# Expert rows fetched in pairs: one indexed DMA for U and V, shared slots, and coefficients for every two picks

## The chip, the cores and the metric

The kernel runs on one core of one Trainium2 chip. Its time is the device time of one execution in microseconds (us), the median of several. A profiled execution is one more execution, with a trace of every instruction and every DMA packet. The engines are TensorE (PE, its weight loads apart as PEld), VectorE (DVE), ScalarE (ACT), GpSimd (POOL) and SyncE (SP). DMA work is done by 16 DMA engines.

## What is computed

Two blocks of layers over 256 tokens of width 1024. The first block has two layers, each a mixer (a gated delta rule in layer 0, attention in layer 1) followed by an expert layer. The change touches only the expert layers:

```python
def peer(h, w_query, sub_keys, u_tab, v_tab):
    def block_fn(xb):                                   # 128 tokens
        qry = (xb @ w_query).reshape(P, PEER_HEADS, 2, PEER_HALF)
        s = jnp.einsum('phcd,hckd->phck', qry, sub_keys)
        top_s, top_i = lax.top_k(s, PEER_TOPK)          # 16 of 128 keys, twice
        cand_s = top_s[..., 0, :, None] + top_s[..., 1, None, :]
        cand_i = top_i[..., 0, :, None] * 128 + top_i[..., 1, None, :]
        best_s, pos = lax.top_k(cand_s.reshape(P, 8, 256), PEER_TOPK)
        idx = jnp.take_along_axis(cand_i.reshape(P, 8, 256), pos, axis=-1)
        gate = jax.nn.softmax(best_s, axis=-1)
        act = jax.nn.gelu(jnp.einsum('pd,phkd->phk', xb, u_tab[idx]), approximate=False)
        return jnp.einsum('phk,phkd->pd', gate * act, v_tab[idx])
```

Each token picks 16 experts in each of 8 heads out of 16384. A pick is a row of 1024 float32 of U (4 KB), which is multiplied with the token, and the row of V with the same number, which is added to the sum with a coefficient. U and V are 64 MB each a layer; only the picked rows are read.

## The kernel before

The class `Peer` (line 1356) is one expert layer. It runs twice: `peer_a` over four tiles of 128 tokens (512 tokens, context and latents) and `peer_m` over two. A **unit** is one tile and one head, so there are 32 and then 16 units; a unit has 16 **picks**, and pick g = 16u + s is one gather of 128 rows (one a token) of U and one of V. In all there are 768 picks, 512 KB of U and 512 KB of V each.

Every engine has its own program; they meet at semaphores. For one unit u:

- **VectorE** (`dve`, 1622; `dve_choose`, 1703) chooses the experts of unit u + 2 in 14 small steps, which stand between the dot products of unit u. `dve_dot` (1657) multiplies a U row with the token and sums it (line 1664). `dve_coef` (1667) makes the 16 coefficients of a unit at once from softmax and gelu; it runs after the third dot of the next unit.
- **ScalarE** (`act`, 1519): softmax's exp of unit u + 2 (1587), gelu of all 16 dots of unit u (1545), then 16 diagonal matrices, the identity scaled with a column of coefficients (1551). Between the diagonals it copies what TensorE made for later units (1571, 1575, 1581).
- **TensorE** (`pe_sum`, 1501): for each pick two matmuls of the diagonal with the V row (1515), which add up in two PSUM banks over the tile's eight units. Between them stand the steps of `between`: the transposes of a token tile ("h", line 212), the query products of two chunks ("q", 8 matmuls each, 1473) and the scores against the keys ("s", 1486). They stand in units 0 to 7 of the first expert layer (512 columns in units 0 to 3, 384 after) and 0 to 5 of the second.
- **GpSimd** (`pool`, 1588) issues the gathers: `pool_u` (1604) for pick s of unit u + 1, then `pool_v` (1612) for pick s of unit u, in turn. U rows go to 7 slots of 4 KB a partition, free again after the dot; V rows go to 7 other slots, free again after the matmul. The indices are ready two units ahead. The last three V slots hold the norm's scratch at first, so V's fifth gather waits for the norm of all tiles.
- **SyncE** loads the query weights (1 MB for two chunks) into a ring.

At the start of a layer VectorE takes the norm, chooses unit 0, does six steps of choosing unit 1 and begins with the dots. ScalarE and TensorE do the norm of tile 0, query chunks 0 to 3, the norm of the rest, chunks 4 to 7, and then the units. At the end of a tile `dve_add` (1677) adds the sum to the residual.

## Time and profile before

| | us |
|---|---|
| median of 3 runs | 4846.64 |
| lowest, highest | 4842.84, 4847.74 |
| profiled execution, first to last instruction (its span) | 4732.4 |
| first gather to last sum of `peer_a` | 1381 to 2826 |
| first gather to last sum of `peer_m` | 3009 to 3723 |

| engine | busy, us | share of the span |
|---|---|---|
| TensorE matmul | 3897.4 | 82% |
| VectorE | 2747.9 | 58% |
| GpSimd | 2127.3 | 45% |
| ScalarE | 883.1 | 19% |

For the profiled execution itself there is the span alone; the runs' median lies 114 us above it. Busy shares are averages over stages with different limits, so they are read per stretch. A row of a table of stretches gives the busy time of each engine, the granted TensorE clock as a share of 2.4 GHz, the mean busy share of the 16 DMA engines (it goes a little over 1 where packets overlap) and what they moved.

### The profile page before, as it was taken

What the parts mean: (1) busy time and instruction counts of PE and PEld (TensorE: products, weight loads), DVE (VectorE), ACT (ScalarE), POOL (GpSimd) and SP (SyncE); (2) the same over time, 40 slices, a digit from 0 to 9 for tenths busy, and PEclk for the clock granted to TensorE, in tenths of its full rate; (3) what the DMA queues carried; (4) which work ended last, traced back from release to release, by engine and by line L of the source; (5) the groups of instructions that cost most, each with busy time, mean ns of one, the idle gap of its engine ahead of it and who ended that gap; (6) DMA issues with size and microseconds to landing.
All of it is one profiled execution on the core that took longest, in us unless ns stands there. A gap on an engine that the chain in (4) does not pass through costs nothing.

```text
span 4732.4 us, 41731 instructions
## 1 busy us (share of the span) xinstructions
PE 3897.4 (82%) x14279; PEld 2202.3 (47%) x14279; DVE 2747.9 (58%) x5596; ACT 883.1 (19%) x2101; POOL 2127.3 (45%) x1999
## 2 busy tenths in 40 slices
PE   6799999899978987777777778688777889875999
PEld 1448864598644443322222235444322357532584
DVE  1258872678646666666666635666666247538241
ACT  0233221332212221111111112222111111010100
POOL 1006430255217777777777760377777300018000
PEclk6699999999989999988988999899898889986999
DMA  9310002100149999999999981799999524320343
GB/s 371 126 61 1 1 27 71 54 1 1 44 152 376 378 376 376 391 385 384 406 391 383 386 328 54 255 402 405 404 390 400 204 82 133 129 93 1 121 149 124
DMA packets 380097, 1043.15 MB, mean 220 GB/s; under 512 B 31683, under 2 KB 115885, under 8 KB 379889
## 3 DMA queue, kind: packets, MB, share of 16 engines
q0 software_dynamic: 225424, 816.31, 44.9%
q1 hardware_dynamic: 154464, 224.18, 14.1%
q8 instruction: 117, 1.92, 0.2%
q14 instruction: 92, 0.75, 0.0%
HBM read 1039.29 MB, written 1.08 MB: 220 GB/s over the span
## 4 chain that ended last, share of the span: by engine, by line
PE 47%; POOL 19%; DVE 13%; DMA 12%; issue 8%; ACT 2%; DVEq 0%; POOLq 0%; ACTq 0%
PE psum L261 12%; PE psum L1515 11%; POOL arena L1618 8%; DMA arena<-in_peer_u,arena 7%; POOL arena L1609 7%; PE psum L299 4%; PE psum L717 3%; DMA arena<-in_peer_v,arena 3%; PE psum L756 2%; PE psum L212 2%; PE psum L1037 2%; PE psum L1473 2%; DMA arena<-in_ada_w 2%; POOL arena L1133 2%; PE psum L1026 2%
## 5 line engine op out<-in xcount | busy, mean ns | idle before, releaser
L1515 PE MATMUL psum<-arena 128*128 128x512 f32 x3072 | 1499.4, 636 | 469.7 <-ACT arena L1551 306.8
L1664 DVE SCALAR_TENSOR_TENSOR arena<-arena 128x1024 bf16<-128x1024 f32 x768 | 939.5, 1225 | 674.5 <-DMA arena<-in_peer_u,arena 674.3
L1515 PEld LDWEIGHTS psum<-arena 128*128 128x128 f32 x3072 | 596.1, 203 | 1337.0 <-issue 947.2
L1618 POOL DMA_INDIRECT arena<-in_peer_v,arena x768 | 825.1, 1074 | 273.0 <-issue 173.0
L1609 POOL DMA_INDIRECT arena<-in_peer_u,arena x768 | 780.7, 1017 | 298.6 <-issue 204.4
L261 PE MATMUL psum<-ring,arena 128*128 128x512 f32 (+2 forms) x1408 | 600.2, 590 | 30.1 <-DVE arena L2540 9.1
L261 PEld LDWEIGHTS psum<-ring,arena 128*128 128x128 f32 x1408 | 271.7, 201 | 352.9 <-issue 326.4
L1133 POOL TENSOR_TENSOR arena<-arena 128x512 f32<-128x512 f32 x224 | 283.8, 1292 | 110.0 <-PE psum L1026 70.5
L299 PE MATMUL psum<-arena,ring 128*128 128x256 f32 x1408 | 311.6, 383 | 9.0 <-DVE arena L2535 7.7
L1551 ACT ACTIVATE arena<-consts,arena 128x128 f32<-128x128 f32 x768 | 234.1, 388 | 328.9 <-DVE arena L1674 328.9
L299 PEld LDWEIGHTS psum<-arena,ring 128*128 128x128 f32 x1408 | 268.3, 192 | 50.3 <-issue 8.0
L1124 POOL TENSOR_TENSOR arena<-consts,arena 128x512 f32<-128x512 f32 x32 | 39.2, 1247 | 500.0 <-PE psum L977 472.3
L212 PE MATMUL psum<-consts,arena 128*128 128x128 f32 (+2 forms) x833 | 134.7, 310 | 150.5 <-DVE arena L362 77.5
L717 PE MATMUL psum<-arena,ring 128*128 128x512 f32 x512 | 229.4, 602 | 1.6 <-issue 1.6
L1026 PE MATMUL psum<-arena 128*128 128x128 f32 x1536 | 198.1, 282 | 32.4 <-POOL arena L1133 28.4
L212 PEld LDWEIGHTS psum<-consts,arena 128*128 128x128 f32 (+2 forms) x833 | 109.9, 160 | 208.9 <-issue 107.8
L1026 PEld LDWEIGHTS psum<-arena 128*128 128x128 f32 x1536 | 183.8, 195 | 44.6 <-POOL arena L1133 37.9
L2704 POOL TENSOR_TENSOR arena<-arena 128x256 f32<-128x256 f32 x32 | 32.5, 1017 | 339.7 <-DVE arena L2728 337.1
L1473 PE MATMUL psum<-arena,ring 128*128 128x128 f32 (+3 forms) x704 | 176.7, 408 | 7.9 <-ACT arena L1303 6.2
L1037 PE MATMUL psum<-arena 128*128 128x128 f32 x1536 | 179.4, 275 | 0.0
L1037 PEld LDWEIGHTS psum<-arena 128*128 128x128 f32 x1536 | 175.4, 192 | 0.0
L1099 ACT ACTIVATE arena<-psum 128x512 f32<-128x512 f32 x192 | 114.6, 597 | 286.1 <-PE psum L1026 285.0
(381 smaller groups left out, 3970.5 us busy)
## 6 DMA issues: line engine op xcount, KB each, us to landing
arena<-in_ada_w SPq DMA_DIRECT2D x48, 1024.0 KB, 14.4
ring<-in_ffn_w_up SPq DMA_DIRECT2D x44, 1024.0 KB, 5.1
ring<-in_dn_w_in SPq DMA_DIRECT2D x24, 1024.0 KB, 5.4
ring<-in_peer_w_query SPq DMA_DIRECT2D x22, 1024.0 KB, 7.1
ring<-in_ffn_w_down SPq DMA_DIRECT2D x20, 1024.0 KB, 5.0
arena<-in_peer_u,arena POOLq DMA_INDIRECT x768, 6.5
arena<-in_peer_v,arena POOLq DMA_INDIRECT x768, 6.5
ring<-in_ev_w_in SPq DMA_DIRECT2D x10, 1024.0 KB, 5.2
```

The source lines that it names most:

```text
L212: return e.transpose(out, in_, self.k.const("ident")[0:n, 0:n])
L261: m = e.matmul(o, self.hT[:, k0 + k, t * 128:(t + 1) * 128], w[:, k, :], start=k0 + k == 0, stop=k0 + k == self.KC - 1)
L299: m = e.matmul(self.bank(c)[:, 0:self.nt], w[:, k, j * 128:(j + 1) * 128], self.hT[:, k, 0:self.nt], start=k == 0, stop=k == self.KC - 1)
L717: m = e.matmul(k.banks[j % 4], w[:, q, j % 2 * 128:(j % 2 + 1) * 128], self.hT[:, q, :], start=q == 0, stop=q == 7)
L1026: m = e.matmul(b0[:, h * 128:(h + 1) * 128], gL[:, h, :], Pm[:, h, :], start=True, stop=True)
L1037: m = e.matmul(b1[:, h * 128:(h + 1) * 128], T[:, h, :], Xp[:, h, :], start=True, stop=True)
L1133: e.tensor_tensor(gL, D, rep(self.lev[:, 2 * l + ch[1], :]), MUL).then_inc(*G.up(key(f"lev{l}", ch)))
L1473: m = e.matmul(k.banks[j % 2][:, 0:w_], w[:, n, c % 2 * 128:(c % 2 + 1) * 128], self.hT[:, n, a * 128:b * 128], start=n == 0, stop=n == 7)
L1515: m = e.matmul(k.banks[4 + t % 2 * 2 + nh], self.diag[g % self.ND], self.vsl[g % self.NV][:, nh * 512:(nh + 1) * 512], start=u % 8 == 0 an ...
L1609: e.indirect_dma_start(self.us[g % self.NU], None, self.tables()[0], bass.IndirectOffsetOnAxis(ap=self.eid[u % 6][:, s:s + 1], axis=0)).th ...
L1618: e.indirect_dma_start(self.vsl[g % self.NV], None, self.tables()[1], bass.IndirectOffsetOnAxis(ap=self.eid[u % 6][:, s:s + 1], axis=0)).t ...
L1664: e.scalar_tensor_tensor(self.junk[g % 2], self.us[g % self.NU], 1.0, self.h[:, u // 8, :], MUL, MUL, accum_out=self.a[u % 2][:, s:s + 1]) ...
```

## The change

The tables U and V, two inputs before, are laid side by side as one input `peer_uv` of 8 KB rows. The rest follows from it:

- One gather a pick brings both rows (`pool_rows`), into 8 slots of 8 KB that replace the 7 + 7 of 4 KB. A slot is free after the pick's matmul. GpSimd goes pick by pick, with no unit's lead of U over V. The norm's scratch lies in the last two slots, so the seventh gather waits for the norm.
- Gelu, coefficients and diagonals are made for two picks at a time: ScalarE's gelu takes 2 columns, and VectorE's `dve_coef` stands behind each second dot of the same unit. There are 8 diagonals in place of 16.
- A query product ("q") is cut in halves of four matmuls, "qa" and "qb", after picks 2, 4, 6 and 8; the scores come after 11 and 14. ScalarE's copies have places of their own (`act_steps`). The exp of unit u + 2 moves from the unit's start to its end.
- At the start, VectorE chooses unit 1 whole (14 steps, not 6) and scales tile 3 before the first dot; ScalarE's exp of unit 0 stands before the norm of the rest.

```diff
-    NU, NV, ND = 7, 7, 16
+    NS, ND = 8, 8
...
-        self.us = [k.al(1024) for _ in range(self.NU)]
-        self.vsl = [k.al(1024) for _ in range(self.NV)]
+        self.uv = [k.al(2048) for _ in range(self.NS)]
+        self.us, self.vsl = [a[:, 0:1024] for a in self.uv], [a[:, 1024:2048] for a in self.uv]
...
-            steps.update({3: ("q", j), 7: ("q", j + 1), 9: ("s", j), 12: ("s", j + 1)})
+            steps.update({2: ("qa", j), 4: ("qb", j), 6: ("qa", j + 1), 8: ("qb", j + 1), 11: ("s", j), 14: ("s", j + 1)})
...
+    def act_steps(self, u):
+        steps, j = {}, self.unit_job(u)
+        if self.unit_job(u - 1) is not None:
+            steps[2] = ("s", self.unit_job(u - 1) + 1)
+        if u + 1 < self.nt:
+            steps[4] = ("h", u + 1)
+        if j is not None:
+            steps.update({9: ("q", j), 13: ("q", j + 1), 15: ("s", j)})
+        return steps
...
-            for n in range(8):
+            for n in {"q": range(8), "qa": range(4), "qb": range(4, 8)}[kind]:
...
             e.wait_ge(*S.at(("dg", g)))
-            e.wait_ge(*self.l_v[g % self.NV].at(g))
+            e.wait_ge(*self.l_uv[g % self.NS].at(g))
...
+        self.act_softmax(e, 0)
         self.norm.act_rest(e)
-        self.act_softmax(e, 0)
...
+            for q in range(8):
+                e.wait_ge(*V.at(("dot", 16 * u + 2 * q + 1)))
+                if u >= 2 and q == 0:
+                    e.wait_ge(*V.at(("cf", u - 2, 7)))
+                e.activation(self.ge[u % 2][:, 2 * q:2 * q + 2], self.a[u % 2][:, 2 * q:2 * q + 2], ACT.Gelu, bias=0.0,
+                             scale=1.0).then_inc(*S.up(("gelu", u, q)))
+                e.wait_ge(*V.at(("cf", u, q)))
+                for s in (2 * q, 2 * q + 1):
+                    g = 16 * u + s
+                    if g >= self.ND:
+                        e.wait_ge(*P.at(("y", g - self.ND)))
...
-            for s in range(16):
-                if u + 1 < self.units:
-                    self.pool_u(e, u + 1, s)
-                self.pool_v(e, u, s)
...
+                self.pool_rows(e, u, s)
+
+    def pool_rows(self, e, u, s):
         g = 16 * u + s
+        if g == self.NS - 2:
             e.wait_ge(*self.S.at(("nT", self.nt - 1)))
+        if g >= self.NS:
+            e.wait_ge(*self.P.at(("y", g - self.NS)))
+        e.indirect_dma_start(self.uv[g % self.NS], None, self.table(),
+                             bass.IndirectOffsetOnAxis(ap=self.eid[u % 6][:, s:s + 1], axis=0)).then_inc(*self.l_uv[g % self.NS].up(g))
...
-                for _ in range(6):
+                for _ in range(14):
                     next(steps)
+                if self.nt > 2:
+                    self.norm.dve_scale(e, 3)
...
                 self.dve_dot(e, u, s)
+                next(steps, None)
+                if s % 2:
+                    self.dve_coef(e, u, s // 2)
...
+    given["peer_uv"] = np.concatenate([given.pop("peer_u"), given.pop("peer_v")], axis=2)
```

Where the instructions stand, before and after. In these rows a line number is that of the kernel in question, and "x4" counts instructions of the same form.

TensorE, unit 0 of the first layer, from its first sum (before: 1515 sums, 1473 queries, 1486 scores):

```order
L1515 MATMUL psum<-arena 128x512 x4
L212 MATMUL psum<-consts,arena 128x128 x8
L1515 MATMUL psum<-arena 128x512 x4
L1473 MATMUL psum<-arena,ring 128x512 x8
L1515 MATMUL psum<-arena 128x512 x8
L1473 MATMUL psum<-arena,ring 128x512 x8
L1515 MATMUL psum<-arena 128x512 x4
L1486 MATMUL psum<-arena 128x128 x4
```

The same place after the change (1529 sums, 1487 queries, 1500 scores):

```order
L1529 MATMUL psum<-arena 128x512 x4
L212 MATMUL psum<-consts,arena 128x128 x8
L1529 MATMUL psum<-arena 128x512 x2
L1487 MATMUL psum<-arena,ring 128x512 x4
L1529 MATMUL psum<-arena 128x512 x4
L1487 MATMUL psum<-arena,ring 128x512 x4
L1529 MATMUL psum<-arena 128x512 x4
L1487 MATMUL psum<-arena,ring 128x512 x4
L1529 MATMUL psum<-arena 128x512 x4
L1487 MATMUL psum<-arena,ring 128x512 x4
L1529 MATMUL psum<-arena 128x512 x6
L1500 MATMUL psum<-arena 128x128 x4
```

The query products stand in four groups of four with two picks between them; they were two groups of eight.

ScalarE, two units late in the first layer, before (1587 exp, 1545 gelu, 1551 diagonals):

```order
L1587 ACT_TABLE_LOAD
L1587 ACTIVATE arena<-arena 128x16
L1545 ACT_TABLE_LOAD
L1545 ACTIVATE arena<-arena 128x16
L1551 ACTIVATE arena<-consts,arena 128x128 x16
```

And after, the end of one unit and the beginning of the next (1604 exp, 1557 gelu, 1564 diagonals):

```order
L1557 ACTIVATE arena<-arena 128x2
L1564 ACTIVATE arena<-consts,arena 128x128 x2
L1604 ACT_TABLE_LOAD
L1604 ACTIVATE arena<-arena 128x16
L1557 ACT_TABLE_LOAD
L1557 ACTIVATE arena<-arena 128x2
L1564 ACTIVATE arena<-consts,arena 128x128 x2
L1557 ACTIVATE arena<-arena 128x2
L1564 ACTIVATE arena<-consts,arena 128x128 x2
```

Exp, with both table loads, now stands between the last diagonals of one unit and the first gelu of the next, and gelu comes eight times a unit.

VectorE, the first dots of unit 0 after the change (1664 dot, 1673 and 1676 coefficient, the rest choosing):

```order
L1344 TENSOR_SCALAR arena<-x_res,arena 128x1024
L1664 SCALAR_TENSOR_TENSOR arena<-arena 128x1024
L1695 MAX arena<-arena 128x8
L1697 MAX_INDEX arena<-arena 128x8
L1664 SCALAR_TENSOR_TENSOR arena<-arena 128x1024
L1699 MATCH_REPLACE arena<-arena 128x128
L1701 MAX arena<-arena 128x8
L1673 RECIPROCAL arena<-arena 128x1
L1676 SCALAR_TENSOR_TENSOR arena<-arena 128x2
```

The scaling of tile 3 stood behind the fourth dot; the first coefficient stood behind the third dot of unit 1.

## Rows read from the trace of the kernel before

**Rows 1.** The page's costliest groups: busy us, mean ns | idle before, its releaser.

```profile
L1515 PE MATMUL psum<-arena 128*128 128x512 f32 x3072 | 1499.4, 636 | 469.7 <-ACT arena L1551 306.8
L1664 DVE SCALAR_TENSOR_TENSOR arena<-arena 128x1024 bf16<-128x1024 f32 x768 | 939.5, 1225 | 674.5 <-DMA arena<-in_peer_u,arena 674.3
...
L1551 ACT ACTIVATE arena<-consts,arena 128x128 f32<-128x128 f32 x768 | 234.1, 388 | 328.9 <-DVE arena L1674 328.9
```

**Rows 2.** Table of stretches: PE, PEld, DVE, ACT, POOL busy; PEclk, DMA share, GB/s.

```profile
1850.00:2790.00 940.00, 696.56 (x1392) 270.60 (x1390) 616.96 (x1422) 162.86 (x439) 727.26 (x691) 0.90 1.01 390
3270.00:3690.00 420.00, 315.46 (x671) 127.11 (x672) 273.67 (x626) 74.08 (x206) 321.61 (x316) 0.91 1.02 400
...
2270.00:2340.00 70.00, 51.72 (x102) 20.19 (x101) 48.94 (x114) 15.74 (x42) 52.24 (x51) 0.89 1.03 407
1500.00:1660.00 160.00, 153.21 (x407) 72.58 (x406) 99.14 (x234) 35.71 (x86) 114.33 (x111) 0.98 1.00 380
2750.00:2760.00 10.00, 5.40 (x12) 1.73 (x10) 4.93 (x8) 0.21 (x1) 7.56 (x9) 1.00 1.03 410
...
2060.00:2070.00 10.00, 5.45 (x7) 2.33 (x8) 6.38 (x16) 5.89 (x17) 7.56 (x9) 0.52 1.02 408
```

**Rows 3.** DMA view of 50:90 (2 KB rows), 3665:3695 and 3660:3700 (gathers).

```profile
DMA packets 7782, 15.46 MB, mean 386 GB/s; under 512 B 235, under 2 KB 235, under 8 KB 7782
...
DMA packets 3366, 12.26 MB, mean 409 GB/s; under 512 B 375, under 2 KB 375, under 8 KB 3365
...
arena<-in_peer_v,arena POOLq DMA_INDIRECT x20, 7.8
```

**Rows 4.** Timeline of GpSimd, in a clean stretch: start, us, what.

```profile
2741.56 1.01 POOL L1609 DMA_INDIRECT arena<-in_peer_u,arena  x1 [0.30 <-issue]
2742.88 0.94 POOL L1618 DMA_INDIRECT arena<-in_peer_v,arena  x1 [0.30 <-issue]
```

**Rows 5.** Table of stretches: start and end of each expert layer.

```profile
1380.00:1434.00 54.00, 13.57 (x81) 12.66 (x82) 41.19 (x111) 12.53 (x38) 28.23 (x24) 0.61 0.77 257
2796.00:2826.00 30.00, 29.36 (x68) 12.84 (x68) 0.40 (x2) 4.83 (x17) 11.90 (x13) 1.00 0.70 267
3009.00:3053.00 44.00, 17.74 (x80) 15.00 (x78) 39.76 (x110) 6.28 (x17) 28.33 (x26) 0.70 0.92 320
3694.00:3723.00 29.00, 29.00 (x68) 12.62 (x67) 0.40 (x2) 4.78 (x16) 9.98 (x11) 1.00 0.68 253
```

**Rows 6.** Timeline of the first layer's start: start, us, engine, line.

```profile
1371.51 0.29 DVE L1692 MAX8 arena<-arena 128x8 f32<-128x128 f32 x1 [3.26 <-ACT arena L1575]
...
1381.11 1.06 POOL L1609 DMA_INDIRECT arena<-in_peer_u,arena  x1 [20.15 <-DVE arena L1741]
...
1394.62 0.75 DVE L1344 TENSOR_SCALAR arena<-x_res,arena 128x1024 f32<-128x1024 f32 x1
...
1411.34 0.28 ACT L1575 ACTIVATE arena<-psum 128x128 f32<-128x128 f32 x1 [0.35 <-PE psum L1486]
...
1433.79 6.35 PE L1515 MATMUL psum<-arena 128*128 128x512 f32 x8 [22.48 <-ACT arena L1551]
```

**Rows 7.** Line 1609, U's gathers: from issue to landing.

```profile
DMA to landing us min/median/max: 4.3/6.5/12.5
```

**Rows 8.** Timeline of a quiet unit's boundary: table load, coefficient, sum.

```profile
2007.84 1.28 ACT L1545 ACT_TABLE_LOAD   x1
...
2063.83 0.23 DVE L1674 SCALAR_TENSOR_TENSOR arena<-arena 128x16 f32<-128x16 f32 x1
...
2064.55 8.01 PE L1515 MATMUL psum<-arena 128*128 128x512 f32 x11 [6.96 <-ACT arena L1551]
```

**Rows 9.** Timeline of TensorE in unit 0: a query product, four picks.

```profile
1444.29 7.03 PE L1473 MATMUL psum<-arena,ring 128*128 128x512 f32 x16
1451.15 7.03 PE L1515 MATMUL psum<-arena 128*128 128x512 f32 x16
```

**Rows 10.** DMA view of 171.6:174.8, around the load of line 677.

```profile
DMA packets 188, 1.00 MB, mean 312 GB/s; under 512 B 27, under 2 KB 45, under 8 KB 188
```

110 lines of the change are left out of this document (41 added, 69 removed).

## The prediction

> **What bounds the kernel now.** I began with the costliest groups of the page [rows 1]. The dearest two lie in the expert layers: the diagonal matmuls (line 1515) and the dot products (line 1664). Both idle long: TensorE 470 us, VectorE 674.5 us of 674.5 for a landing U row. So the data sets the pace, if anything does.
>
> The second view is the table of stretches [rows 2]. In two quiet stretches, with hardly any other load, the DMA engines are busy for 1.01 and 1.02 of the time and move 390 and 400 GB/s. In the cleanest one they move 407 to 409 at 1.03 (here and below 409, [rows 2, 3]). TensorE is busy for 74% to 75% of the quiet stretches, VectorE for 66%. A pick is 128 tokens x 8 KB = 1.0486 MB, so 409 GB/s is 2.564 us a pick, 390 is 2.689, 400 is 2.621. Only units 0 to 3 of the first expert layer differ: TensorE is busy for 153.2 of 160 us there.
>
> GpSimd is almost as tight: 691 gathers, busy for 727 us and with 0.30 us of gap before each, fill 934 of the 940 us of the first quiet stretch [rows 2, 4]. One gather costs it 0.94 + 0.30 us, so two cost 2.49 us a pick against 2.564 of the DMA engines. [rows 4] shows the pair repeating every 2.56 us, the U gather stretched to 1.01. I read that as a queue that pushes back: the DMA engines are the bound and GpSimd has 3% in hand.
>
> **One 8 KB row in place of two 4 KB rows.** Bytes stay; the number of rows read halves. Rows of other lengths give the price [rows 3]: loads in 2 KB rows run at 386 GB/s, gathers of 4 KB rows at 409, both at a share above 1. Spread over 16 engines that is 84.9 ns and 160.2 ns of one engine for a row: 75.3 ns for 2 KB more, and some 9.6 ns that belong to the row and not to its bytes. An 8 KB row is then 160.2 + 150.6 = 310.8 ns instead of 320.4. Eight rows an engine and pick: 77 ns, 2.564 becomes 2.487 us (422 GB/s). It counts for the picks that the DMA engines pace, 768 less the 64 of units 0 to 3: 704 x 0.077 = **54 us**. The bounds are 0, if a row is cut into two packets, and 54.
> The row shows 9.6 ns that do not scale. The Trainium skill, DMA: Bandwidth & Descriptors, section Why small descriptors are slow, names about 3 cycles between the two halves of a DMA engine, at the 850 MHz of its bandwidth section 3.5 ns, so an estimate by that page would be 704 x 8 x 3.5 ns = 20 us. The trace has the larger number beside it and decides.
>
> **Slow stretches.** From 409 down to 390 and 400 GB/s is 0.125 us for each of 448 picks and 0.057 for each of 256: 56 + 15 = 71 us [rows 2]. At 390 the share is still 1.01, so packets take longer there and it is hardly a matter of idle engines. What comes with each read should halve; what comes with each byte stays; and GpSimd, which issues once a pick now (1.25 of 2.49 us), can refill after a stall, which it could not. Bounds 0 and 71. I take a third, **24 us**, nearer the end of no gain, because the share stays near 1.
>
> **Start and end of each expert layer.** Against 409 GB/s the four stretches at the ends lose, by their rates in [rows 5], 54 x (1 - 257/409) = 20, 30 x (1 - 267/409) = 10, 44 x (1 - 320/409) = 10 and 29 x (1 - 253/409) = 11: 51 us. The cause at the start is that no V slot is freed before all 16 dots of unit 0, gelu and coefficient are done: first sum at 1433.79, 52.7 us after the first gather [rows 6].
> After the change, first layer: choose(1) runs whole before the first dot. choose(0) took from 1371.51 until just before GpSimd's first gather at 1381.11, 9.3 us, so choose(1) ends at 1390.1 and the scaling of tile 3 at 1390.9, where it now ends at 1395.4: 4.5 us earlier. All behind it moves with it: ScalarE's last copy of pair 6 (1411.34) comes at about 1407. Gelu's table load 1.28, gelu, coefficient, diagonal and a first matmul at the low clock put the first freed slot at 1412.5. Eight slots are full at 1381 + 3 + 8 x 2.49 = 1404, and new data lands from 1415: a gap of 11. With 3 us of first landing (4.3, the least of [rows 7], less 1.3 of transfer) and an end of 6.5 (dot 1.3, gelu, coefficient and diagonal 1.1, two picks of 1.72 and their handovers): 20.5 us. Second layer: it has no tile 3 to wait for, and its query loads fill the gap beside the 8 gathers; the softmax that now stands ahead of the norm's rest costs at most a table load and exp. As an estimate 3 + 1 + 6.5 = 10.5. Sum 31, taken as 33; gain 51 - 33 = **18 us**, bounds 5 and 25.
>
> **The new chain.** U and V share a slot, so a slot is free only after landing, dot, gelu, coefficient, diagonal and matmul. For the even pick of a pair: its partner lands 2.49 later, dot and the reading of its sum about 1.3, VectorE's step of choose 0.66 (9.3/14; a gelu on two columns hides under it), coefficient 0.23, diagonal 0.39, matmuls 1.96 (1.72 behind another pick, [rows 9]), handovers 0.3 as an estimate: 7.3 us [rows 1, 6, 8]. Behind it GpSimd's wait and issue, 1.25, and the landing, 4.3 + 1.25 for the doubled bytes at least: 14.1 us against 8 x 2.49 = 19.9 that eight slots cover. Slack 5.8 us.
> What eats of it, one at a time: the unit's end on ScalarE, exp (two short instructions, 0.4 as an estimate) with its table load and gelu's, 1.28 + 0.4 + 1.28 = 3.0 us [rows 8], mostly over before the next pair's dots are done; dve_add, four instructions on 512 columns, half a dot each, 2.6 us as an estimate; a query half on TensorE, half of 6.86 = 3.4 us [rows 9]. All fit. Only in units 0 to 3 do four halves and a transposition come within eight picks: 8 x 1.72 + 13.7 + 0.9 = 28.4 us of TensorE against 21 us of data, a lag of 7. I charge 2 us for each of those units and 2 for the rest: **-10 us**, bounds 0 and -40.
> TensorE in units 0 to 3 needs 16 x 1.72 + 2 x 6.86 + 0.9 + 0.9 + 0.9 = 44 us a unit, DMA 16 x 2.49 + 3.0 for the query load (1024 rows of 1 KB at 84.9 - 37.7 = 47 ns on 16 engines) = 42.8: no gain there, in halves or whole. TensorE's clock: in 2750 to 2760 it is busy for 5.4 of 10 us at a granted clock of 1.00, 2.4 GHz; in 2060 to 2070, with an idle of 6.96 us in it, it stands at 0.52, near 1.2 GHz [rows 2, 8]. The change takes that wait at each unit's start away and leaves gaps of about 1.6 us a pair, so I cost the clock at 0.
> VectorE: 16 x 1.3 + 9.3 + 8 x 0.23 + 0.2 = 32.1 of 40 us a unit, seven more coefficient instructions, under the data. Eight instead of 16 diagonals: ScalarE could be no more than 8 slots ahead anyway, 0.
>
> **The sum.** 54 + 24 + 18 - 10 = 86 us off the profiled span of 4732.4, so 4646. The median of the runs is 114 us above that span; nothing of the change lies in what is outside, so 4846.6 - 86 = **4761 us**.
>
> **Rivals.**
> *A row is cut.* If GpSimd writes two packets of 4 KB for each row, the rate stays, and it may pay for 256 of them. For it: all gathers of before are 4 KB, none shows an 8 KB one. Against it: around the load of line 677, 7 KB a partition from the same queue, 188 packets carry 1.00 MB, on average 5.3 KB, so packets above 4 KB exist [rows 10]. The first term is 0 and of the second 4 stay: 4 + 18 - 10 = 12 us, 4835. The Trainium skill, DMA: Bandwidth & Descriptors, section SWDGE vs HWDGE vs iDMA, gives a packet of at most 4096 B as preferred; by that rule the forecast falls to this one; for a direct load the row of line 677 speaks against it, for an indirect one no row here shows it. Chance 0.15.
> *The slow stretches go.* If GpSimd without room was their cause, all 71 us come back: 54 + 71 + 18 - 10 = 133, 4714. Against it: the share stays at 1.01 in the stretch that loses most. Chance 0.12.
> *The chain paces: slower.* If a doubled gather lands as late as the latest before, 12.5 + 1.25 us [rows 7], the chain is 7.3 + 1.25 + 13.8 = 22.3 us, 2.79 a pick. Before it was (448 x 2.689 + 256 x 2.621)/704 = 2.664. 704 x 0.126 = 89 lost, 18 won: 4918. It decides from a landing of 8 x 2.664 - 8.55 = 12.8 us on. For it: one queue of slots now feels each stop of three engines. Against it: in a saturated stretch a gather lands after 7.8 us [rows 3], which is 9.1 with the doubled bytes and leaves 2.3 us; and a late landing there is queueing, which shrinks when fewer are in flight. Chance 0.15.
>
> **How the numbers follow.** Forecast 0.58, at 4761, its own range 4735 to 4800. About 0.2%, 9.7 us, is what a measurement of this kernel can tell from no change: 4837 to 4856. Faster: 0.58 + 0.12 + 0.10 of the cut rows = 0.80; same: 0.05; slower 0.15. For 8 in 10 the range goes from 4722, which leaves half of the better rival out, to 4852, which leaves most of the slower one out.
>
> **What would show it.** Packets of the gathers' queue: half as many, near 8 KB (cut: as many as before). Rate in quiet stretches: 403 to 418 GB/s at a share above 1 (chain: a share of 0.95 or less, with GpSimd waiting for TensorE and the DMA queue running empty). GpSimd busy for under 45% there. First sum of the first layer at about 1411 and its end 50 to 60 us earlier than 2826; first diagonal wait of each unit gone; TensorE's clock at or near 1.00. I am wrong if landings rise over 12 us, if units 0 to 3 take over 50 us each (47 before), or if a gather of 8 KB rows costs GpSimd 1.9 us.

## The result and the profile after

| | before | after |
|---|---|---|
| median of 4 runs, us | 4846.51 | 4609.55 |
| lowest, highest | 4842.84, 4847.74 | 4607.80, 4614.34 |
| span of the profiled execution | 4732.4 | 4607.3 |
| that execution's own time | not known | 4609.08 |

The changed kernel takes 0.9515 of the time of the kernel before, with a 95% interval of 0.9502 to 0.9529: 237 us less. Forecast were 86 less, at 4761, with a range that ended at 4722. The sign was right, the size was wrong by a factor of almost three, and the time lies outside the range.

Two things stand out before any reading. The spans differ by 125 us only, so 112 of the 237 us are not to be found by laying these two traces side by side. And the profiled execution of after ran for 1.8 us more than its span, where the prediction put 114 us outside the span.

The costliest groups of after, on its page (as [rows 1]: busy us, mean ns | idle before, its releaser), then its gathers' queue (packets, MB, share of 16 engines) and the median from issue to landing:

```profile
L1529 PE MATMUL psum<-arena 128*128 128x512 f32 x3072 | 1447.0, 615 | 401.6 <-ACT arena L1564 398.1
L1664 DVE SCALAR_TENSOR_TENSOR arena<-arena 128x1024 bf16<-128x1024 f32 x768 | 941.5, 1226 | 518.8 <-DMA arena<-in_peer_uv,arena 479.4
L1622 POOL DMA_INDIRECT arena<-in_peer_uv,arena x768 | 866.0, 1128 | 1170.9 <-PE psum L1529 1029.8
...
q0 software_dynamic: 114832, 816.26, 43.4%
...
arena<-in_peer_uv,arena POOLq DMA_INDIRECT x768, 12.8
```

VectorE still waits for rows, but for 479.4 us in place of the 674.3 of [rows 1]. GpSimd has turned from an engine that is never free into one that waits 1030 us for a slot (a matmul of line 1529). And a gather now lands 12.8 us after its issue, where [rows 7] had 6.5.

Stretches of after (busy us of each engine, then TensorE's clock, DMA share, GB/s): the start of the first layer, units 0 to 3, a quiet stretch, the middle of either layer, and the other three ends:

```profile
1381.00:1434.00 53.00, 36.93 (x140) 22.67 (x141) 34.03 (x102) 17.51 (x51) 15.35 (x15) 0.81 0.84 314
1500.00:1660.00 160.00, 154.72 (x412) 73.50 (x412) 110.16 (x277) 42.27 (x115) 63.48 (x59) 1.00 1.00 407
1850.00:2650.00 800.00, 592.35 (x1248) 231.12 (x1247) 587.02 (x1468) 195.67 (x545) 358.60 (x311) 0.98 1.01 415
...
1434.00:2703.00 1269.00, 1015.60 (x2334) 424.65 (x2332) 905.95 (x2254) 321.66 (x891) 559.87 (x493) 0.98 1.01 413
2960.00:3570.00 610.00, 482.61 (x1161) 210.44 (x1159) 428.59 (x1064) 150.78 (x432) 266.85 (x237) 0.97 1.01 416
...
2703.00:2733.00 30.00, 22.20 (x48) 8.62 (x48) 13.48 (x26) 5.14 (x17) 4.15 (x5) 1.00 0.61 252
2917.00:2960.00 43.00, 37.18 (x137) 26.11 (x138) 29.21 (x96) 10.99 (x30) 15.07 (x15) 0.92 0.95 357
3570.00:3600.00 30.00, 22.37 (x49) 8.62 (x48) 14.32 (x28) 5.38 (x18) 4.74 (x5) 1.00 0.64 266
```

The middles of the same two layers before, whole and not only the quiet parts that [rows 2] shows:

```profile
1434.00:2796.00 1362.00, 1079.18 (x2372) 449.53 (x2372) 881.56 (x2044) 258.00 (x679) 1035.47 (x988) 0.92 1.00 387
3053.00:3694.00 641.00, 503.40 (x1197) 224.31 (x1198) 415.73 (x963) 121.65 (x333) 491.84 (x477) 0.92 1.02 399
```

The rate rose from 387 to 413 and from 399 to 416 GB/s. From its first gather to its last sum the first layer took 1445 us before (1381 to 2826) and 1351 now (1382.0 to 2732.9); the second took 713.6 and now 682.6 (2917.6 to 3600.2). That is 94 and 31 us, together 125, which is the whole difference of the spans.

The cleanest stretch of after, 2670 to 2700, in the view of the DMA engines, and the dots in a piece behind it (start, us, what, idle before):

```profile
DMA packets 1739, 12.67 MB, mean 422 GB/s; under 512 B 193, under 2 KB 193, under 8 KB 193
```

```profile
2701.20 1.23 DVE L1664 SCALAR_TENSOR_TENSOR arena<-arena 128x1024 bf16<-128x1024 f32 x1 [1.26 <-DMA arena<-in_peer_uv,arena]
...
2703.68 1.23 DVE L1664 SCALAR_TENSOR_TENSOR arena<-arena 128x1024 bf16<-128x1024 f32 x1 [0.76 <-DMA arena<-in_peer_uv,arena]
...
2706.16 1.23 DVE L1664 SCALAR_TENSOR_TENSOR arena<-arena 128x1024 bf16<-128x1024 f32 x1 [1.25 <-DMA arena<-in_peer_uv,arena]
```

All packets but 193 are rows of 8 KB in one piece: 1546 x 8192 B are 12.66 of the 12.67 MB. At 422 GB/s over 16 engines such a row takes 310.6 ns, and a dot starts every 2.48 us.

The start of the first layer (start, us, what, idle before), as [rows 6]:

```profile
1382.01 1.06 POOL L1622 DMA_INDIRECT arena<-in_peer_uv,arena  x1 [20.15 <-DVE arena L1744]
...
1396.24 0.94 POOL L1622 DMA_INDIRECT arena<-in_peer_uv,arena  x1 [6.89 <-ACT arena L1303]
...
1407.02 1.28 ACT L1557 ACT_TABLE_LOAD   x1
...
1409.39 5.37 PE L1529 MATMUL psum<-arena 128*128 128x512 f32 x8 [2.70 <-ACT arena L1564]
...
1413.28 1.05 POOL L1622 DMA_INDIRECT arena<-in_peer_uv,arena  x1 [14.85 <-PE psum L1529]
```

The seventh gather waits for the norm, the first sum comes at 1409.39 in place of 1433.79, and the ninth gather, the first into a freed slot, starts at 1413.28.

### The profile page after: what moved, and what is told of

Same layout as the page of the kernel before. It is cut to its first block, busy times and chain, and to the rows that moved or that the text cites. A ratio compares the mean times of both kernels' runs of the same rounds, so it can differ in the third digit from the quotient of the medians.

```text
span 4607.3 us, 42013 instructions
## 1 busy us (share of the span) xinstructions
PE 3848.6 (84%) x14279; PEld 2181.3 (47%) x14279; DVE 2793.2 (61%) x5932; ACT 987.5 (21%) x2441; POOL 1388.5 (30%) x1231
## 4 chain that ended last, share of the span: by engine, by line
PE 49%; DMA 25%; DVE 15%; POOL 5%; issue 3%; ACT 3%; DVEq 0%; POOLq 0%; ACTq 0%
DMA arena<-in_peer_uv,arena 23%; PE psum L261 13%; PE psum L1529 10%; PE psum L299 4%; PE psum L717 4%; PE psum L1487 3%; PE psum L756 2%; DVE arena L1664 2%; PE psum L212 2%; PE psum L1037 2%; DMA arena<-in_ada_w 2%; PE psum L1026 2%; POOL arena L1133 2%; DVE arena L1175 1%; DVE arena L1222 1%
## 5 line engine op out<-in xcount | busy, mean ns | idle before, releaser
L1529 PE MATMUL psum<-arena 128*128 128x512 f32 x3072 | 1447.0, 615 | 401.6 <-ACT arena L1564 398.1
L1664 DVE SCALAR_TENSOR_TENSOR arena<-arena 128x1024 bf16<-128x1024 f32 x768 | 941.5, 1226 | 518.8 <-DMA arena<-in_peer_uv,arena 479.4
L1622 POOL DMA_INDIRECT arena<-in_peer_uv,arena x768 | 866.0, 1128 | 1170.9 <-PE psum L1529 1029.8
L1529 PEld LDWEIGHTS psum<-arena 128*128 128x128 f32 x3072 | 568.8, 194 | 1230.1 <-ACT arena L1564 648.3
L1557 ACT ACTIVATE arena<-arena 128x2 f32<-128x2 f32 x384 | 78.2, 204 | 1241.8 <-DVE arena L1664 1241.7
L1564 ACT ACTIVATE arena<-consts,arena 128x128 f32<-128x128 f32 x768 | 268.3, 394 | 224.2 <-DVE arena L1676 221.1
L1026 PEld LDWEIGHTS psum<-arena 128*128 128x128 f32 x1536 | 184.8, 196 | 43.7 <-POOL arena L1133 37.1
L1037 PEld LDWEIGHTS psum<-arena 128*128 128x128 f32 x1536 | 175.4, 192 | 0.0
L1222 DVE TENSOR_TENSOR arena<-arena,psum 128x512 f32<-128x512 f32 x192 | 126.4, 666 | 60.4 <-PE psum L1037 60.1
## 6 DMA issues: line engine op xcount, KB each, us to landing
arena<-in_peer_uv,arena POOLq DMA_INDIRECT x768, 12.8
```

Of the source, the lines that this page charges most:

```text
L1026: m = e.matmul(b0[:, h * 128:(h + 1) * 128], gL[:, h, :], Pm[:, h, :], start=True, stop=True)
L1037: m = e.matmul(b1[:, h * 128:(h + 1) * 128], T[:, h, :], Xp[:, h, :], start=True, stop=True)
L1529: m = e.matmul(k.banks[4 + t % 2 * 2 + nh], self.diag[g % self.ND], self.vsl[g % self.NS][:, nh * 512:(nh + 1) * 512], start=u % 8 == 0 an ...
L1564: e.activation(self.diag[g % self.ND], k.const("ident"), ACT.Copy, bias=0.0, scale=self.cf[u % 2][:, s:s + 1]).then_inc(*S.up(("dg", g)))
L1622: e.indirect_dma_start(self.uv[g % self.NS], None, self.table(), bass.IndirectOffsetOnAxis(ap=self.eid[u % 6][:, s:s + 1], axis=0)).then_i ...
L1664: e.scalar_tensor_tensor(self.junk[g % 2], self.us[g % self.NS], 1.0, self.h[:, u // 8, :], MUL, MUL, accum_out=self.a[u % 2][:, s:s + 1]) ...
```

## Experiments

Four questions were open. Is it the row's length or the structure around it? What was slow in the stretches below the ceiling? How many slots, and what length of the chain, does the new rate need? And where are the 112 us that no pair of these traces shows? Kernels with the same letter (A to F) ran on one chip and share its runs of the kernel before.

| kernel | built from | chip | time, us | before there | ratio, 95% interval |
|---|---|---|---|---|---|
| before_again | before | A | 4764.39 | 4763.59 | 0.9989 to 1.0025 |
| two4k | after, two 4 KB gathers | A | 4673.89 | 4763.59 | 0.979 to 0.985 |
| slots6 | after, 6 slots | A | 4740.54 | 4763.59 | 0.9945 to 0.9978 |
| wholeq | after, whole query products | A | 4608.31 | 4763.59 | 0.9649 to 0.9708 |
| after_again | after | B | 4605.68 | 4854.35 | 0.9471 to 0.9502 |
| fullpool | after, GpSimd kept busy | B | 4883.38 | 4854.35 | 1.0041 to 1.0075 |
| shortdots | before, short dots | B | 4811.95 | 4854.35 | 0.9901 to 0.9934 |
| slots7 | after, 7 slots | B | 4630.32 | 4854.35 | 0.9524 to 0.9560 |
| two4k_b | as two4k | C | 4674.51 | 4761.62 | 0.9806 to 0.9855 |
| slots59 | before, 5 U and 9 V slots | C | 4749.47 | 4761.62 | 0.996 to 1.0001 |
| coef4 | after, groups of four | C | 4770.51 | 4761.62 | 1.0008 to 1.0037 |
| two4k_c | as two4k | D | 4676.51 | 4759.94 | 0.9805 to 0.9856 |
| coef1 | after, groups of one | D | 4601.99 | 4759.94 | 0.9651 to 0.9694 |

**before_again.** The kernel before, unchanged.

> The kernel before, unchanged. The profiled execution of it that the prediction was made from had a span of 4732, while its timed runs took 4843 to 4848; the changed kernel's span of 4607 lies only 2 us under its own run. Theory 'uneven gathers': the gathers of 4 KB rows have slow stretches whose amount differs between executions, and the profiled one was a lucky one; then the span here lies anywhere between 4730 and 4846 and follows its own run's time within 3 us, and the DMA rate in the quiet stretches falls with it (390 GB/s at 4732, some 365 at 4845). Rival 'outside': 112 us of the kernel before lie outside what the trace covers; then the span is again about 4732 beside a run of 4846.

It took 4764.39 us, and the profiled execution 4756.96 beside a span of 4754.9. Every profile whose own time is on record behaves so: the time is the span and 1.8 to 2.1 us. So nothing of any size lies outside a trace. (Of the first profile of the kernel before, with its span of 4732.4, the own time is not known; it is taken to be like the others.) The quiet stretch ran at 386 GB/s, and the page gives the gathers (as [rows 1]):

```profile
1850.00:2600.00 750.00, 539.99 (x1088) 209.88 (x1088) 500.62 (x1172) 134.02 (x358) 581.19 (x546) 0.91 1.00 386
```

```profile
L1618 POOL DMA_INDIRECT arena<-in_peer_v,arena x768 | 849.0, 1105 | 266.6 <-issue 160.9
L1609 POOL DMA_INDIRECT arena<-in_peer_u,arena x768 | 786.6, 1024 | 298.8 <-issue 199.5
```

With these means of the whole kernel a pick costs GpSimd 1.105 + 1.024 us and twice the 0.30 of [rows 4], 2.73 us. 1.0486 MB in 2.73 us is 384 GB/s: the rate that the stretch has, to within 1%. In the clean stretch of [rows 4] it was 1.01 + 0.94, 2.56 us and 409 GB/s.

**two4k.** The structure of after with the gathers of before:

```diff
-        e.indirect_dma_start(self.uv[g % self.NS], None, self.table(), ...
+        for half, n in ((self.us, "peer_u"), (self.vsl, "peer_v")):
+            e.indirect_dma_start(half[g % self.NS], None, ...)
```

> The changed kernel with everything kept but the row: each pick is fetched by two gathers of 4 KB rows, from separate U and V, into the two halves of its slot. Theory 'row': the 8 KB row carries the gain (fewer, longer packets, fewer stalls); then this takes 4780 to 4860, near the kernel before. Theory 'room and chain': the gain comes from the new order (coefficients for every two picks, start and end) and 8 shared slots; then this takes 4610 to 4700. By the prediction's terms alone (packet 54 us, ends 18 us) it would be 4609 + 54 = 4663 to 4690.

4673.89 us. The stretch 1850 to 2600 and the gathers:

```profile
1850.00:2600.00 750.00, 548.32 (x1134) 214.26 (x1133) 535.96 (x1338) 175.46 (x491) 573.71 (x565) 0.96 1.02 400
```

```profile
L1623 POOL DMA_INDIRECT arena<-in_peer_u,arena x768 | 767.3, 999 | 305.7 <-issue 171.5
L1623 POOL DMA_INDIRECT arena<-in_peer_v,arena x768 | 798.5, 1040 | 234.1 <-issue 232.9
```

After itself was not timed on chip A; wholeq (below), which differs from it only in the query products, took 4608.31 there, and after took 4605.7 to 4609.6 on two other chips. So of the 155 us between before and wholeq on this chip, 90 come with the structure alone (shared slots, groups of two, the earlier start) and 66 with the single gather of 8 KB rows. That one gather both shortens the DMA engines' work and halves GpSimd's issues; this run does not part the two. GpSimd's price again gives the rate: 0.999 + 1.040 + 0.60 = 2.64 us, 397 GB/s, measured 400. The structure makes the gathers cheaper for GpSimd, by 0.09 us a pick against before_again; why it does was not separated.

**two4k_b and two4k_c** are the same kernel again, to see whether it varies from chip to chip as before does.

> The changed kernel with two gathers of 4 KB rows a pick, as before, on another chip. On the chip where the kernel before took 4764 it took 4674. Theory 'GpSimd paces at two gathers a pick': no room to run ahead, so it shifts with the chip as the kernel before does: if the latter is at 4850, this is at 4720 to 4760. Rival 'only the order matters for the spread': it stays at 4665 to 4685.

> The changed kernel, but with two gathers of 4 KB rows for each pick, from two tables, into the halves of the shared slot. 4674 on the chips on which before takes about 4762. Where before takes about 4850: theory A (the loss grows as the bytes in flight shrink) lets this kernel, with 2.8 MB in flight, lose as well, some 50 to 80 us, to 4725 to 4755; theory B (the loss belongs to stages that the change doesn't touch, or to the old order of the engines) leaves it at 4675 within 10 us.

They took 4674.51 and 4676.51 us, but before took 4761.62 and 4759.94 there. That settles the size of the step and not the question: how two4k fares on a chip on which before takes 4850 is not known.

**slots6 and slots7.** Depth of the queue, everything else as after:

```diff
-    NS, ND = 8, 8
+    NS, ND = 6, 8        # slots7: 7, 8
```

> The changed kernel with 6 slots of 8 KB in place of 8. Theory 'slack': eight slots cover 8 x 2.49 = 19.9 us against a chain of at least 14.1, so six (14.9 us) just about cover it, with no room for the unit boundaries: 4640 to 4760. Rival 'already slot bound': the DMA queue ran at a share of 1.01 only because eight are enough by a hair; then six cost the ratio, 16 x 2.49 x 8/6: 4609 + 0.6 us x 768 = 5070 or so.

> The changed kernel with 7 slots of 8 KB. With 6 it took 4740, with 8 it takes 4609. Theory 'depth absorbs unevenness': what a slot is worth falls off, so 7 gives 4630 to 4660, with a quiet rate of 405 to 412 GB/s. Rival 'straight line': 4675, half way.

4740.54 and 4630.32 us, against 4605 to 4610 with eight. The quiet stretch of slots6, then of slots7:

```profile
1850.00:2600.00 750.00, 551.62 (x1110) 215.64 (x1108) 522.13 (x1312) 172.95 (x483) 327.28 (x278) 0.94 0.99 393
```

```profile
1850.00:2600.00 750.00, 556.68 (x1170) 217.35 (x1171) 551.78 (x1387) 183.65 (x513) 325.57 (x293) 0.97 1.01 415
```

With six slots the DMA share is 0.99 and the rate 393 although the rows are 8 KB long: without the slots 8 KB rows bring only 23 us against before. With seven the quiet stretches are whole (415, above the 405 to 412 that were expected) and what is lost lies in the busy units: 387 GB/s in 1500 to 1660, where after has 407. The medians from issue to landing were 8.6 and 10.7 us.

**wholeq.** The query products in one piece again, after picks 3 and 7:

```diff
-            steps.update({2: ("qa", j), 4: ("qb", j), 6: ("qa", j + 1), 8: ("qb", j + 1), 11: ...
+            steps.update({3: ("q", j), 7: ("q", j + 1), 11: ...
```

> The changed kernel with whole query products (eight matmuls, after picks 3 and 7) in place of halves. Theory 'halves matter little': TensorE lags in units 0 to 3 of the first layer by whole products, 3.4 us more at a time, 2 to 4 us a unit: 4612 to 4630. Rival 'no effect': within 3 us of 4609.

4608.31 us, where after took 4605.68 and 4609.55 on other chips. With eight slots the halves are worth nothing that these runs can measure.

**after_again and fullpool.** After once more, and after with one GpSimd addition on 512 columns of a spare buffer behind each gather, which uses up the time that the change frees on that engine and touches nothing else:

```diff
+        if self.units * 16 > g + 8:
+            e.wait_ge(*self.G.now())
+            e.tensor_tensor(self.spare, self.k.cv[:, 0:512], self.k.cv[:, 0:512], ADD).then_inc(*self.G.up())
```

> The changed kernel, unchanged, as the control of this group beside the kernel before on the same chip. Theory 'uneven gathers': the kernel before differs from chip to chip (4843 to 4848 in one place, 4747 to 4775 in another), the changed one does not: 4600 to 4620 here, whatever the kernel before takes. Rival: the changed kernel shifts with it, by a third or more of the shift.

> The changed kernel with one more instruction of GpSimd behind each gather, an addition on 512 columns of constants into a spare buffer that nobody reads (1.29 us as in the trace of before). GpSimd then needs 1.25 + 1.3 + gap, some 2.6 us a pick, as in the kernel before, while rows stay 8 KB and the DMA engines need 2.49. Theory 'GpSimd paces': the kernel before ran at GpSimd's own pace (two gathers of 1.045 + 0.30 us are 2.69 a pick, and 390 GB/s is 2.69 a pick); then this loses the gain of the feed: 2.6 to 2.9 us a pick, 4690 to 4800. Rival 'rows': GpSimd's room doesn't matter, 4610 to 4640.

After_again took 4605.68 us on a chip on which before takes 4854.35. Fullpool took 4883.38, more than the 4690 to 4800 that were expected. Its stretch, and line 1623 in it (durations in ns as least, median, most; then what GpSimd waited for, in us and times):

```profile
1850.00:2600.00 750.00, 534.63 (x1009) 208.57 (x1008) 704.94 (x1187) 156.18 (x438) 702.68 (x507) 0.90 0.98 359
```

```profile
L1623 POOL DMA_INDIRECT arena<-in_peer_uv,arena x254: 958/1770/2042, 1849.4 to 2599.6; - x127
its engine sat idle before it (us, times) until:
  issue: 35.5, 225
  PE psum L1530: 4.5, 10
...
DMA to landing us min/median/max: 6.2/6.7/12.6
```

GpSimd is full again: 750 us for 254 gathers is 2.95 us each, 355 GB/s, measured 359. Eight slots stand ready and it cannot fill them; the landing falls back to 6.7 us, since few gathers are under way. A GpSimd that is never free is rebuilt here in the kernel of after, and it gives back all of the gain on this chip and more. A reserve on GpSimd is necessary. The addition did more than wait, though: it stretches gathers (median 1.77 us) and VectorE (704.94 us busy in the stretch against 551 to 552), so the run shows the direction, not a price for each microsecond of GpSimd.

**shortdots.** The other way round, in the kernel before: the dots over 64 of 1024 columns, so that VectorE hardly works beside the gathers. The dot products and with them the coefficients are other numbers; everything else is done.

```diff
-        e.scalar_tensor_tensor(self.junk[g % 2], self.us[g % self.NU], 1.0, self.h[:, u // 8, :], ...
+        e.scalar_tensor_tensor(self.junk[g % 2][:, 0:64], self.us[g % self.NU][:, 0:64], 1.0, self.h[:, u // 8, 0:64], ...
```

> The kernel before with dot products over 64 of the 1024 columns, so the coefficients, not the expert numbers of the layer at hand, are wrong; all gathers stay. VectorE is then almost idle beside its choosing. Theory 'GpSimd is stretched by VectorE': the gathers' mean on GpSimd falls from 1.05 to 0.95 to 0.97 us, the rate in quiet stretches rises from 386 or 390 to 405 or more, time 40 to 80 us under the kernel before. Rival 'the queue pushes back': the gathers' mean on GpSimd stays at 1.03 to 1.05, the rate at 385 to 395, and only the units' starts gain a little: 0 to 20 us under the kernel before.

4811.95 us, 42 less than before, as the theory had it; the gathers' mean came as expected too, the rate of 405 or more did not. The stretch, and the waits of GpSimd in it (us in total, times, longest):

```profile
1850.00:2600.00 750.00, 531.31 (x1056) 202.47 (x1054) 216.60 (x1126) 126.48 (x336) 498.16 (x525) 0.91 0.98 372
```

```profile
POOL arena L1618 <- issue: 83.5, 222, 3.2
POOL arena L1609 <- issue: 68.9, 226, 0.3
POOL arena L1618 <- PE psum L1515: 43.6, 22, 4.1
POOL arena L1618 <- remote: 38.2, 13, 4.6
```

A gather now takes GpSimd 498.16/525 = 0.95 us. So VectorE's work is what stretches it in before. A fuller queue is not: the typical gather takes the same in before, where rows land after 6.5 us, and in after, where they land after 13.1 (1850 to 2600; least, median, most in ns):

```profile
L1609 POOL DMA_INDIRECT arena<-in_peer_u,arena x275: 941/947/1976, 1849.4 to 2598.4; - x138
```

```profile
L1622 POOL DMA_INDIRECT arena<-in_peer_uv,arena x292: 942/947/1974, 1851.2 to 2598.2; - x146
```

The means lie above these medians because some gathers take almost twice as long. But the rate in shortdots is only 372. There is no trace of before from chip B; on chip F, where it takes about as long (4843), it has 368, so next to nothing was gained: in place of its own pace GpSimd meets the V slots (43.6 us for a sum, and 38.2 that the view puts down to "remote", a release whose record it lacks). The kernel before has no second reserve behind the first. GpSimd's pace alone is therefore not the explanation; a reserve in its time and slots to use it are wanted together.

**slots59.** Before, with the slots shared out otherwise, since V's seven are what is met at a unit's boundary:

```diff
-    NU, NV, ND = 7, 7, 16
+    NU, NV, ND = 5, 9, 16
```

> The kernel before with 5 U and 9 V slots in place of 7 and 7. Theory 'the stop at each unit': TensorE waits some 7 us for the coefficients of a unit, the V slots fill up and GpSimd, with one queue for both, stops for a V slot while U slots are free; two more V slots take that stop away: 20 to 60 us under the kernel before. Rival 'GpSimd's own pace': within 10 us of the kernel before, or slower for want of U slots.

4749.47 us, 12 less, and the interval touches 1. The quiet stretch still has 386 GB/s at 581.78 us of GpSimd, so there the wait at each unit's boundary was nearly free. Units 0 to 3 are another matter:

```profile
1500.00:1660.00 160.00, 159.93 (x432) 76.29 (x431) 106.04 (x249) 37.23 (x91) 121.78 (x116) 1.00 1.03 402
```

The six profiles of before have 365 to 380 GB/s there. In these units the seven V slots were short. It is one profile, and with five U slots the layer's start is slower (229 GB/s from 1381 to 1434, where before_again has 258).

**coef4 and coef1.** The length of the chain by which a slot comes free, with eight slots: gelu, coefficients and diagonals for four picks, and for one.

```diff
-            for q in range(8):
-                e.wait_ge(*V.at(("dot", 16 * u + 2 * q + 1)))
+            for q in range(4):                                      # coef1: range(16)
+                e.wait_ge(*V.at(("dot", 16 * u + 4 * q + 3)))       # coef1: 16 * u + q
...
-                if s % 2:
-                    self.dve_coef(e, u, s // 2)
+                if s % 4 == 3:                                      # coef1: after every dot
+                    self.dve_coef(e, u, s // 4)
```

> The changed kernel with coefficients for every four picks in place of two. By the chain of the prediction the first pick of a group then waits for three partners: 7.3 + 5 + two more matmuls ahead of the freed slots, so 14.1 us becomes some 19 to 20 against the 19.9 that eight slots cover. Theory 'depth': fewer gathers stand queued, landing falls from 12.8 to about 8 us, and the time goes to 4640 to 4720, like six or seven slots. Rival 'chain is slack': within 10 us of the changed kernel.

> The changed kernel with gelu, coefficient and diagonal made for every single pick, so that the even pick of a pair need not wait for its partner: its slot comes free some 2.5 us earlier, against eight more gelus and eight more coefficient instructions a unit. Theory: the queue is deep enough with groups of two and the DMA engines are the bound at 415 to 419 GB/s, so the quiet stretches stay within 3 GB/s and the time within 15 us of 4608, in either direction. Rival: the length of the chain still costs (groups of four lost 160 us, seven slots lost 21), then more slots are in flight and the rate goes to 420 or more, the time to 4595 or less. Other rival: ScalarE and VectorE with twice as many short instructions pace units 0 to 3, then it is 4625 or more.

Groups of four took 4770.51 us, far above the 4640 to 4720 that were expected: all of the gain is gone, with 8 KB rows, eight slots and GpSimd idle for more than half of the time. Groups of one took 4601.99, 4 to 8 less than after has on other chips, so slightly the better kernel; the two were not timed on one chip. The quiet stretch of coef4, then that of coef1 with its units 0 to 3:

```profile
1850.00:2600.00 750.00, 555.80 (x1074) 228.28 (x1073) 501.58 (x1206) 148.28 (x403) 295.87 (x269) 0.86 0.97 383
```

```profile
1500.00:1660.00 160.00, 159.15 (x429) 76.41 (x428) 116.40 (x314) 52.82 (x149) 71.10 (x61) 1.00 1.02 415
...
1850.00:2600.00 750.00, 580.23 (x1169) 205.25 (x1168) 568.78 (x1527) 228.18 (x656) 332.21 (x293) 0.98 1.01 414
```

In coef4 slots come free four at a time, the DMA share is 0.97 at 383 GB/s, and TensorE's granted clock is 0.86 where after has 0.98. In coef1 the quiet stretch gains nothing, 414 against 414 to 415. Units 0 to 3 do, 415 against 407, and the rival by which the doubled short instructions pace them is out. The chain of after is short enough outside these units.

**before_third to before_sixth.** The kernel before, one profile each, on chips C, D, E and F, until one came on which it takes as long as in the first runs.

> The kernel before, unchanged, for one more profile beside its own time on this chip. Two chips gave 4764 and 4854. If this one is slow again (4840 or more), the profile shows where the 90 us are. Theory 'depth': all of it lies in the two expert layers, as a lower rate in the quiet stretches (370 to 378 GB/s against 386 to 390) at a DMA share of 0.97 to 1.00, with more packets over 1.5 times the median; nothing elsewhere moves by more than 5 us. Rival 'clock or compute': the other layers are longer as well.

> The kernel of before, unchanged, for one more profile. Open is where some 90 us lie by which its time differs from chip to chip (about 4760 on some, 4846 to 4854 on another) while the changed kernel stays at 4605 to 4610. If this chip is one on which it takes about 4850: theory A, packets take longer or stall more while few bytes are in flight: the quiet stretches 1850 to 2600 and 3150 to 3450 show 375 GB/s or less at a share still near 1.00, GpSimd still full with gathers, and the two expert layers together are about 80 us longer than in the first profile. Theory B, the 90 us lie outside the expert layers: the expert layers keep their length, 386 to 400 GB/s, and other stages are longer. If it is one on which it takes about 4760, the span is 4733 to 4757 and nothing is told apart.

> The kernel of before, unchanged, for a profile on another chip: the fourth profile of it came from a chip on which it takes 4760 and told nothing apart. If it takes about 4850 here: theory A, the 90 us more lie in the expert layers, with the quiet stretches 1850 to 2600 and 3150 to 3450 at 375 GB/s or less at a share near 1.00 and GpSimd as full as before; theory B, they lie outside the expert layers, and these show 386 to 400 GB/s. If it takes about 4760, the span is 4733 to 4770 and nothing is told apart.

> The kernel of before, unchanged, once more on whichever chip comes: if it takes about 4850, theory A (the 90 us more lie in the expert layers: quiet stretches at 375 GB/s or less, GpSimd full) against theory B (they lie outside, the quiet stretches show 386 to 400 GB/s). If it takes about 4760, nothing is told apart and the place of the 90 us stays open.

The first three took 4754.97, 4771.61 and 4759.39 us and told nothing new. The fourth took 4843.37, with a span of 4841.5. Its stretches: before the first expert layer; the first layer; the quiet stretch; the second layer:

```profile
0.00:1381.00 1381.00, 1230.52 (x6784) 857.56 (x6784) 798.46 (x1230) 326.38 (x666) 378.26 (x336) 0.93 0.21 71
...
1381.00:2895.00 1514.00, 1129.25 (x2520) 474.66 (x2520) 921.14 (x2156) 274.18 (x729) 1103.76 (x1024) 0.91 0.96 362
...
1850.00:2600.00 750.00, 520.13 (x1033) 199.22 (x1032) 473.30 (x1109) 127.84 (x343) 561.10 (x519) 0.90 0.98 368
...
3077.00:3832.00 755.00, 559.03 (x1344) 252.91 (x1343) 455.26 (x1074) 132.72 (x366) 541.29 (x512) 0.90 0.97 367
```

All that precedes the expert layers ends at 1381 as in the first profile. The first layer takes 1514 us in place of 1445 and the second 755 in place of 714: 69 + 41 = 110 of the 109.1 us between the spans. So on chip F the difference is found: it is the same loss in the same place, larger. That the 112 us of the first chip are the same is an inference from the like times (4843 and 4846); no trace of an execution that took 4846 there is on record. How it looks from near, in two stretches of 20 us of that execution:

```profile
2070.00:2090.00 20.00, 8.41 (x17) 3.21 (x18) 11.28 (x26) 2.86 (x8) 12.30 (x14) 0.86 0.91 329
...
2110.00:2130.00 20.00, 12.29 (x26) 4.07 (x24) 13.54 (x30) 1.81 (x4) 13.35 (x13) 1.00 0.90 326
```

In each of these 20 us the DMA engines are busy for only 0.90 or 0.91; in the 20 us between them they move 404 GB/s. In the wait view for 1850 to 2600 GpSimd stands behind such moments:

```profile
POOL arena L1618 <- remote: 24.1, 10, 3.7
POOL arena L1618 <- PE psum L1515: 20.8, 36, 4.0
```

It waits for a V slot, by up to 4 us at a time, which in a kernel with seven of them I read as one late transfer with the slots behind it full. Of the 750 us, busy time and gaps of 0.30 leave 750 - 561.10 - 519 x 0.30 = 33 us of such waits; in the quiet stretch of [rows 2] the same sum leaves 5 of 940. The packets of the traces, in 1850 to 2600, show late rows too: those over three times the median are 0.8% in before, 1.4% in before_sixth and 0.3% in two4k; of the 8 KB rows 0.2% in after and slots7, but 1.9% in fullpool, on the same chip as slots7. So they come with a short supply and not with the chip alone; whether they are its cause or its effect, and why some chips have more of them, no run shows.

## Why the prediction was wrong, step by step

**The 114 us outside the span: the step that failed.** The prediction took the distance between the profiled span and the runs' median as something that "lies outside" and that the change leaves alone. Nothing lies there: a run is its span and 2 us. The 4732.4 us belong to a quick execution, whose time of some 4734 is 9 us below the lowest of all the runs of before that were timed since (4743.4), and the median of 4846.6 to a chip that I take to be like F, on which the same program loses 109 us more in its expert layers. The carried-over 114 us were thus, but for 2, part of what the change removes. Taken alone this misses 112 us of the 151.

**One 8 KB row: right.** Predicted 310.8 ns, 2.487 us a pick and a ceiling of 422 GB/s; measured 310.6 ns, 2.48 us and 422. I count it for all 768 picks and not for 704, since the rate rose in units 0 to 3 too (380 to 407): 59 us, not 54. The 9.6 ns of a row are borne out (160.2 and 310.6 ns give 9.8). The Trainium skill, DMA: Bandwidth & Descriptors, section Why small descriptors are slow, names about 3 cycles for each packet; the estimate from it, 3.5 ns, was too small by this measure. The Trainium skill, DMA: Bandwidth & Descriptors, section SWDGE vs HWDGE vs iDMA, prefers packets of at most 4096 B. This trace shows indirect gathers in single packets of 8 KB, at 422 GB/s.

**Slow stretches: mis-sized.** 24 us were taken of 71. The loss itself was read too small, as it was taken from the two quiet stretches alone: over the middles of the layers it is 1362 x (1 - 387/409) + 641 x (1 - 399/409) = 89 us. After, against 422, 1269 x (1 - 413/422) + 610 x (1 - 416/422) = 36 are left. So 53 came back on this pair of spans, and some 110 more on a chip like F. The rival "the slow stretches go" had the mechanism and was given 0.12. What spoke against it, the share of 1.01, was a wrong argument: in before_sixth the share is still 0.98 in a stretch that runs at 368. Fullpool shows it best: there GpSimd cannot issue more, and the share is 0.98 at 359 GB/s. As an estimate from its row, a row of 8 KB keeps an engine busy for 16 x 0.98 x 8192 B / 359 GB/s = 358 ns; in after it is 16 x 1.01 x 8192 / 415 = 319. A slow packet counts as a busy engine, and so a share near 1 does not say that the engines have enough under way.

The misreading began a paragraph earlier, at [rows 4]. GpSimd filled 934 of 940 us, and the prediction took the clean pair of 2.56 us as its price and the full engine as a queue that pushes back. The rows of the stretch itself said otherwise: 727.26/691 = 1.05 us and 0.30, 2.70 us a pick, is 388 GB/s, and 390 was measured. Fullpool and two4k have the same equality. It proves little alone, as an engine that is held up by a full queue would show it as well. What tells the two apart is shortdots, in which less work on VectorE made the gathers short (0.95 us), and after, in which a queue twice as deep leaves the typical gather at 0.947. GpSimd could not run ahead, and after a late transfer it could not catch up.

**Starts and ends: the start right, the sum too large.** The first sum came at 1409.39 and the gather into the freed slot at 1413.28; predicted was a freed slot at 1412.5. The four ends lose 53 x (1 - 314/422) + 30 x (1 - 252/422) + 43 x (1 - 357/422) + 30 x (1 - 266/422) = 43 us, not 33: each end of a layer still costs 11 to 12, where 6.5 were taken. Gain 8, not 18.

**The new chain: -10 taken, about 0.** Units 0 to 3 run at 407 GB/s where 380 were, and coef1 shows that only they have something left. The bound of 12.8 us of landing from which the slower rival was to decide was reached as a median, and nothing was lost. The late landing is now the depth of the queue: GpSimd fills freed slots at once and the rows wait in line (12.8 us at 414 GB/s are 5.3 MB under way; before it was 6.5 us at 387, 2.5 MB). "I am wrong if landings rise over 12 us" was thus a bad sign to choose. The rival's arithmetic was sound as a warning: coef4, with a chain two picks longer, takes 9 us more than before.

**Query halves, the clock.** The halves cost nothing and bring nothing (wholeq). The clock was costed at 0; it rose from 0.90 to 0.98 in the quiet stretch, in which TensorE is busy for 74% either way and waits. Nothing here speaks against 0, and no run tests it alone.

**The sum.** 59 + 53 + 8 + 0 = 120 of the 125 us between the spans; predicted 86. The other 112 I put down to the chip, by before_sixth.

What stays open: why the structure of two4k makes a gather 0.09 us a pick cheaper, what makes transfers late on some chips, and whether two4k, slots6 and coef4, which ran only where before takes 4760, would lose more elsewhere.

## What to carry to other kernels

Where one engine issues the transfers, compute its price per item from the stretch in question, gaps included, and lay the rate that follows beside the measured one. If they agree, this engine may be the bound, however near to 1 the DMA share is; then change its price alone and see whether the rate follows. A stream that is near its ceiling needs three reserves together (issue time, buffers, and a short chain that frees them one or two at a time); here six slots gave back 132 us and seven 25, groups of four some 160, two gathers a pick (GpSimd full) 66, and an addition behind each gather, which also slows VectorE, 278. And before a sum is carried from a span to a median, ask which execution the span is from: the distance between the two may be the very loss that the change removes.

## What the runs showed of the hardware

- An indirect gather of 128 rows costs GpSimd the same for 4 and 8 KB rows: a least of 0.94 us and a gap of 0.30. Beside VectorE's work some gathers take up to 2 us and the mean is 1.00 to 1.15 us; with that work cut down it is 0.95.
- Rows of 8 KB go as one packet, 310.6 ns of one engine, 422 GB/s; rows of 4 KB reach 409. From the two lengths some 10 ns belong to each row.
- The rate by what is under way (median landing x quiet rate, estimates from the rows above and the profiles' pages): 2.5 MB, 384 to 390 GB/s; 2.8 MB (two4k), 400; 3.4 MB (slots6), 393; 3.6 MB (coef4, landing 9.3 us), 383; 4.4 MB (slots7), 415; 5.3 MB (after), 414; 6.2 MB (coef1, landing 15.0 us), 414. Beyond some 4.4 MB more depth brings nothing in a quiet stretch. Below it the mean depth alone does not set the rate: coef4, whose slots come free four at a time, is behind two4k with more under way.
- A DMA share near 1 is no proof of a full stream: 0.98 was read at 359 (fullpool), 368 (before_sixth) and 372 GB/s (shortdots), 1.01 at 415 (after).
- The kernel that lives from hand to mouth shows the chip: before took 4743 to 4777 us on four chips (A, C, D, E) and 4841 to 4862 on the others, and its runs on chip A or C scatter over 30 us. The deep one took 4602.6 to 4614.3 in all its runs, on the first chip and B; its near relatives took 4606 to 4610 on A (wholeq) and 4601 to 4603 on D (coef1).
